# A hybrid attention and Mamba-2 decoder step in fp32: moving Pool's page loads and masks around the sample stage, and the order of products and DVE work at the scan's end and in the feed-forward openings

## What is computed

```python
for i in range(DEPTH):                       # DEPTH = 2
    hp, hs = rms_norm(xp, norm_mix[i]), rms_norm(xs, norm_mix[i])
    if i % N_MIXERS == 0:                    # native sparse attention
        yp, ... = nsa_layer(hp, 0, empty, ...)
        y_s, ... = nsa_layer(hs, past_len, past_c, past_s, cache_kv_win[l], ...)
    else:                                    # Mamba-2, chunked scan
        yp, ... = ssd_layer(hp, ...)
        y_s, ... = ssd_layer(hs, state_conv[l], state_ssm[l], ...)
    xp, xs = xp + yp, xs + y_s
    xp = xp + swiglu(rms_norm(xp, norm_ffn[i]), w_gate, w_up, w_down)
    xs = xs + swiglu(rms_norm(xs, norm_ffn[i]), w_gate, w_up, w_down)
```

## Time and profile before

| | before |
|---|---|
| median of 3 runs | 2317.47 us (2316.64 to 2322.97) |
| profiled execution | 2316.88 us |
| its span, granted clock of PE | 2315.2 us, 0.961 |
| busy: PE, weight loads, DVE, ACT, POOL | 2170.0, 1712.9, 1323.0, 519.2, 799.6 us |
| instructions | 33747 |
| moved by DMA | 236.59 MB, 102 GB/s in the mean |

### The profile page before, as it was taken

One profiled execution on the slowest core, in us unless ns is written; L12 is line 12 of the kernel. 1 busy time (PEld: TensorE's weight loads), 2 busy tenths in 40 slices (PEclk: granted clock), 3 DMA queues, 4 the chain that ended last, 5 costly groups with the idle time before them and its releaser, 6 DMA issues.

```text
span 2315.2 us, 33747 instructions
## 1 busy us (share of the span) xinstructions
PE 2170.0 (94%) x11958; PEld 1712.9 (74%) x11958; DVE 1323.0 (57%) x2172; ACT 519.2 (22%) x1197; POOL 799.6 (35%) x702
## 2 busy tenths in 40 slices
PE   8999899997898679999999999999987999999999
PEld 6867677875675457888887878887555878888877
DVE  4457788655774135556642178877986345556312
ACT  2202102104685212111100032233670021111000
POOL 3331000003002743434334245554882433434242
PEclk8999999987898889999999999999997999999999
DMA  4235433304013961711112312221431111122122
GB/s 170 73 110 155 131 119 105 115 13 147 19 38 107 346 231 55 253 74 73 73 50 100 123 61 73 81 85 61 164 147 52 76 73 73 73 89 83 50 77 87
DMA packets 87735, 236.59 MB, mean 102 GB/s; under 512 B 11441, under 2 KB 60722, under 8 KB 73234
## 3 DMA queue, kind: packets, MB, share of 16 engines
q1 hardware_dynamic: 66722, 191.97, 23.2%
q0 software_dynamic: 7024, 29.90, 3.9%
q10 hardware_dynamic: 13824, 12.59, 1.7%
HBM read 217.95 MB, written 23.73 MB: 104 GB/s over the span
## 4 chain that ended last, share of the span: by engine, by line
PE 74%; DVE 13%; issue 5%; POOL 2%; ACT 2%; POOLq 2%; SPq 1%; ACTq 0%; DMA 0%; DVEq 0%
PE ps L340 57%; PE ps L1008 6%; PE ps L1523 2%; PE ps L1536 1%; PE ps L1556 1%; POOLq L1840 1%; DVE sbuf L2534 1%; PE ps L921 1%; SPq L848 1%; PE ps L570 1%; PE ps L1411 1%; DVE sbuf L1156 1%; DVE sbuf L1165 1%; DVE sbuf L1164 1%; DVE sbuf L1162 1%
## 5 line engine op out<-in xcount | busy, mean ns | idle before, releaser
L340 PE MATMUL ps<-sbuf 128*128 128x272 f32 x6048 | 1414.6, 396 | 40.4 <-issue 11.1
L340 PEld LDWEIGHTS ps<-sbuf 128*128 128x128 f32 x6048 | 1156.6, 192 | 297.0 <-issue 20.6
L390 POOL TENSOR_TENSOR sbuf<-sbuf 128x512 f32<-128x512 f32 (+2 forms) x90 | 135.4, 1505 | 736.9 <-PE ps L340 521.7
L359 ACT ACTIVATE sbuf<-ps 128x272 f32<-128x272 f32 x180 | 71.6, 398 | 1118.0 <-PE ps L340 1086.2
L1008 PE MATMUL ps<-sbuf 128*128 128x256 f32 (+1 forms) x1280 | 298.0, 392 | 5.8 <-ACT sbuf L1086 5.0
L1008 PEld LDWEIGHTS ps<-sbuf 128*128 128x128 f32 x1280 | 243.7, 192 | 57.9 <-ACT sbuf L1086 5.4
L370 DVE TENSOR_TENSOR sbuf<-sbuf,ps 128x272 f32<-128x272 f32 x90 | 39.4, 438 | 252.4 <-PE ps L340 251.5
L399 POOL TENSOR_TENSOR sbuf<-sbuf 128x512 f32<-128x512 f32 (+2 forms) x90 | 142.0, 1577 | 7.8 <-PE ps L340 1.0
L396 POOL TENSOR_TENSOR sbuf<-sbuf 128x512 f32<-128x512 f32 (+2 forms) x90 | 136.2, 1513 | 12.3 <-DVE sbuf L407 5.3
L391 POOL TENSOR_TENSOR sbuf<-sbuf 128x512 f32<-128x512 f32 (+2 forms) x90 | 134.4, 1493 | 7.1
L378 DVE TENSOR_TENSOR sbuf<-sbuf,ps 128x272 f32<-128x272 f32 x90 | 39.4, 438 | 126.3 <-PE ps L340 125.5
(11 more groups left out here) (372 smaller groups left out, 2238.1 us busy)
## 6 DMA issues: line engine op xcount, KB each, us to landing
sbuf<-w_gu SPq DMA_DIRECT2D x44, 1024.0 KB, 4.9
sbuf<-w_down SPq DMA_DIRECT2D x32, 704.0 KB, 5.3
sbuf<-cmp_pages SPq DMA_DIRECT2D x160, 128.0 KB, 2.4
sbuf<-w_ssd_in SPq DMA_DIRECT2D x20, 1024.0 KB, 4.8
sbuf<-cmp_pages ACTq DMA_DIRECT2D x96, 128.0 KB, 3.0
sbuf<-w_nsa_in SPq DMA_DIRECT2D x9, 1024.0 KB, 4.9
sbuf<-sel_k SPq DMA_DIRECT2D x64, 128.0 KB, 2.7
sbuf<-sel_v SPq DMA_DIRECT2D x64, 128.0 KB, 4.7
```

Of the source, the lines that this page charges most:

```text
L340: last = pe.matmul(ps[:, bank_of(u, j), 0:HALF], a[:, kt * P:(kt + 1) * P], b[:, kt], start=kt == 0, stop=kt == kts - 1)
L359: do(act.activation(dst, bank_in(u, j), ACT.Copy), f_copied)
L390: do(pool.tensor_tensor(sv[:, 0], a21, a22, ALU.add), f_sums)
```

## The change

It moves work in eight places; the instructions are nearly all the same ones; one small ACT instruction, which loads a table, is new.

1. `p3_pool`: the V pages of sequence 1 are issued behind the compressed-score sums of tile 1, not ahead of them.
2. Sample stage: `comb` gets memory of its own, mask 0 is made before the meeting, the 16 issues of K pages of sequence 3 stand between meeting and memsets; the page numbers are read before the wait and not behind it; K pages of later pairs go ahead of window values on SP; the last constants are loaded earlier; in pair 0 DVE and ACT do the pages' scores ahead of the window's.
3. Feed-forward opening, both passes: (0, 0), (0, 1), (1, 0), (1, 1), and only then strips and (0, 2); POOL's sums wait for the later of products 3 and 4.
4. First down unit: slots released at product 4, not 6; product 4 and on wait for all four sums.
5. Entry of the scan: its first turns are made inside the last `ssd_in` unit, and the meeting there goes.
6. End of the scan: another order of DVE's work, all squares of the second half in one piece, and ACT's root table loaded ahead.
7. Banks of scan and `ssd_out` are numbered anew to fit.
8. `ssd_out`: product order (0, 0), (1, 0), (0, 1), (1, 1), (0, 4), (0, 6), (0, 3), (0, 5), (0, 2), and DVE makes the moving sums one kind after the other.

The diff, cut to its core:

```diff
         EARLY = [(0, 0), (0, 1), (1, 0), (1, 1)] + [(u, j) for u in range(2) for j in range(2, 7)]
-        early_at = {(U_SSD_OUT + u, j): n for n, (u, j) in enumerate(EARLY)}
+        EARLY_SSD = [(0, 0), (1, 0), (0, 1), (1, 1)] + [(0, j) for j in (4, 6, 3, 5, 2)] + [(1, j) for j in range(2, 7)]
+        early_at = {(u0 + u, j): n for u0, order in [(U_SSD_OUT, EARLY_SSD)] + [(u0, EARLY) for u0 in U_FFN]
+                    for n, (u, j) in enumerate(order)}
+        def pair_of(u):
+            return max(u0 for u0 in (U_SSD_OUT,) + U_FFN if u0 <= u)
         def bank_of(u, j):
             if u < U_NSA_OUT:
                 return (7 * u + j) % 6
             if (u, j) in early_at:
-                return (unit_at[U_SSD_OUT] + early_at[u, j]) % 8
-            return (unit_at[u] + j + (2 if j >= 2 and u in (U_NSA_IN, U_SSD_IN) + U_FFN else 0)) % 8
+                n = early_at[u, j]
+                return (unit_at[pair_of(u)] + n + (2 if n >= 4 and pair_of(u) in U_FFN else 0)) % 8
...
             if user is not None:
-                pool.wait_ge(f_mm, multiplied(user, 4))
+                pool.wait_ge(f_mm, max(multiplied(user, 3), multiplied(user, 4)))
...
-            pool.wait_ge(a_vev, 5)
-            pool.wait_ge(stored, 16)
-            p4_load_unit(pool, "V", 1)
             for i in range(1, QT):
                 pool.wait_ge(pc_low, added(i))
                 cmp_sloped(pool, pool_do)
                 cmp_shifted(pool, pool_do, i)
                 cmp_scaled(pool, pool_do, i)
-            meet(pool, 1)
+                if i == 1:
+                    pool.wait_ge(a_vev, 5)
+                    pool.wait_ge(stored, 16)
+                    p4_load_unit(pool, "V", 1)
...
             for pr in range(PAIRS - 1):
+                p4_load_unit(sp, "V", 2 * pr + 2, lambda: sp.wait_ge(ss_mm, pr + 1))
                 sp.wait_ge(sw_mm, pr + 1)
                 win_part(pr + 1, k_half, wk_in)
-                sp.wait_ge(ss_mm, pr + 1)
-                p4_load_unit(sp, "V", 2 * pr + 2)
-                sp.wait_ge(ss_pv, pr + 1)
+                if pr + 2 < PAIRS:
+                    p4_load_unit(sp, "K", 2 * pr + 4, lambda: sp.wait_ge(ss_pv, pr + 1))
+                else:
+                    sp.wait_ge(ss_pv, pr + 1)
                 win_part(pr + 1, v_half, wv_in)
-                if pr + 2 < PAIRS:
-                    p4_load_unit(sp, "K", 2 * pr + 4)
...
+            act.wait_ge(s_comb, 2)
+            def win_exp(pr):
                 act.wait_ge(sw_s, pr + 1)
                 act.activation(Sw, Sw, ACT.Exp, bias=few[:, 4, pr:pr + 1], scale=-1.0,
                                accum_out=few[:, 5, pr:pr + 1]).then_inc(sw_e, 1)
+            def exp(pr):
                 act.wait_ge(ss_s, pr + 1)
                 act.activation(S, S, ACT.Exp, bias=few[:, 8, pr:pr + 1], scale=-1.0,
                                accum_out=few[:, 9, pr:pr + 1]).then_inc(ss_e, 1)
+            for pr in range(PAIRS):
+                for part in (win_exp, exp) if pr else (exp, win_exp):
...
+            def mask(pr):
+                pool.tensor_tensor(comb.rearrange("p (s n) -> p s n", n=SELB), ali.rearrange("p (s n) -> p s n", n=SELB),
+                                   sel_bias[:, pr].unsqueeze(2).to_broadcast([P, NBLK, SELB]), ALU.add).then_inc(s_comb, 1)
+            pool.wait_ge(late_in, 32)
+            pool.wait_ge(sc_dve, SC_DVE["chosen"])
+            mask(0)
+            p4_load_unit(pool, "K", 3, lambda: meet(pool, 1))
             pool.memset(PT[:, NPAGE], 0.0).then_inc(zeroed, 1)
             pool.memset(PTw[:, 4], 0.0).then_inc(zeroed, 1)
             pool.wait_ge(zeroed, 7)
             pool.sem_inc(s_comb, 1)
-            pool.wait_ge(late_in, 16)
-            pool.wait_ge(sc_dve, SC_DVE["chosen"])
-            def mask(pr):
-                pool.tensor_tensor(comb.rearrange("p (s n) -> p s n", n=SELB), ali.rearrange("p (s n) -> p s n", n=SELB),
-                                   sel_bias[:, pr].unsqueeze(2).to_broadcast([P, NBLK, SELB]), ALU.add).then_inc(s_comb, 1)
-            mask(0)
-            p4_load_unit(pool, "K", 3)
             for pr in range(PAIRS - 1):
-                pool.wait_ge(ss_mm, pr + 1)
-                p4_load_unit(pool, "V", 2 * pr + 3)
+                p4_load_unit(pool, "V", 2 * pr + 3, lambda: pool.wait_ge(ss_mm, pr + 1))
                 pool.wait_ge(ss_s, pr + 1)
                 mask(pr + 1)
                 if pr + 2 < PAIRS:
-                    pool.wait_ge(ss_pv, pr + 1)
-                    p4_load_unit(pool, "K", 2 * pr + 5)
+                    p4_load_unit(pool, "K", 2 * pr + 5, lambda: pool.wait_ge(ss_pv, pr + 1))
...
+                    elif v == GU_UNITS and j >= 3:
+                        pe.wait_ge(f_sums, 4 * u + (2 if j == 3 else 4))
+                    elif j == 3:
+                        pe.wait_ge(f_sums, 4 * u + 4)
+                    first = product(pe, u, j, a, b, KH if gu else FH, before)
+                    if j == (4 if v == GU_UNITS else 3) and (v % 2 or not gu):
+                        first.then_inc(w_used, 2 if gu else 4)
+                for v, j in EARLY:
+                    one(v, j)
+                for v in range(2, UNITS_L):
+                    for j in range(7):
+                        one(v, j)
...
+                    if i == ZS + XS - 1 and j == 3:
+                        step_turns(pe)
...
-            group_squares_on(pe, 1, (0, 1))
+            group_squares_on(pe, 1, range(GROUPS))
...
+                if t == N_STEPS:
+                    do(act.activation(cbm_s[:, 0:1], eps, ACT.Sqrt))
...
+            gate(H0_SPREAD - 1)
+            take_state(H0_SPREAD - 1)
+            normed(0)
+            take_y(H0_SPREAD)
+            gate(H0_SPREAD)
+            take_state(H0_SPREAD)
+            normed(1)
+            normed(2)
+            invert_on(dve, do, 1)
+            normed(3)
...
-            invert_on(dve, do, 1)
+            def scaled_half(j):
+                if j % 4 == 0:
+                    dve.wait_ge(g_sp, GROUPS + j // 4 + 1)
+                do(dve.scalar_tensor_tensor(xc[:, j, n2], xc[:, j, n2], ssm_norm[:, j:j + 1],
+                                            ps[:, root_bank(j // 4), 0:HALF], ALU.mult, ALU.mult), g_out)
+            los, his = [xc[:, kt] for kt in range(KT)], [xc[:, KT + kt] for kt in range(KT)]
+            for kt, lo in enumerate(los):
+                scaled_half(kt)
+                do(dve.tensor_tensor(y_t1[:, kt], lo[:, n2], lo[:, n1], ALU.subtract), f_turns)
             for kt in range(KT):
-                for j in (kt, KT + kt):
-                    dve.wait_ge(g_sp, GROUPS + j // 4 + 1)
-                    do(dve.scalar_tensor_tensor(xc[:, j, n2], xc[:, j, n2], ssm_norm[:, j:j + 1],
-                                                ps[:, root_bank(j // 4), 0:HALF], ALU.mult, ALU.mult), g_out)
-                lo, hi = xc[:, kt], xc[:, KT + kt]
-                do(dve.tensor_tensor(y_t1[:, kt], lo[:, n2], lo[:, n1], ALU.subtract))
-                do(dve.tensor_tensor(y_t2[:, kt], hi[:, n2], y_t1[:, kt], ALU.subtract))
+                scaled_half(KT + kt)
+            for kt, hi in enumerate(his):
+                do(dve.tensor_tensor(y_t2[:, kt], hi[:, n2], y_t1[:, kt], ALU.subtract), f_turns)
+            for lo, hi in zip(los, his):
+                do(dve.tensor_tensor(lo[:, n2], hi[:, n2], lo[:, n2], ALU.subtract), f_turns)
+            for kt, hi in enumerate(his):
                 do(dve.tensor_tensor(y_t4[:, kt], hi[:, n1], y_t2[:, kt], ALU.subtract), f_turns)
...
             one(0, 0, half_ready(0))
-            group_squares_on(pe, 1, (2, 3))
-            one(0, 1, half_ready(1))
             for g in range(GROUPS):
-                kt = 4 * (g % 2) + 3
-                claim(pe, root_bank(g), g_out, ST + 2 * kt + 1 + g // 2)
+                claim(pe, root_bank(g), g_out, ST + 4 * g + 4)
             pe.wait_ge(n_r, 5)
             for g in range(GROUPS):
                 pe.matmul(ps[:, root_bank(g), 0:HALF], row_strip(g, 0).to_broadcast([32, P]), rstd[quarter(g), n2],
                           start=True, stop=True).then_inc(g_sp, 1)
             one(1, 0)
+            one(0, 1, half_ready(1))
             one(1, 1)
-            one(0, 2, lambda kt: pe.wait_ge(f_turns, TURNS_BEFORE["ssd_out"] + kt + 1))
-            for i in range(4):
+            one(0, 4, turn_ready(0))
+            one(0, 6, half_ready(3))
+            one(0, 3, turn_ready(1))
+            one(0, 5, turn_ready(2))
+            one(0, 2, turn_ready(3))
+            for i in range(1, 4):
                 for j in range(2 if i < 2 else 0, 7):
-                    if (i, j) != (0, 2):
-                        one(i, j)
+                    one(i, j)
```

236 lines of the change are left out of this document (121 added, 115 removed).

## The result

| | before | changed |
|---|---|---|
| median of 4 runs | 2317.05 us (2314.20 to 2322.97) | 2281.11 us (2277.12 to 2284.75) |
| profiled execution, its span | 2316.88, 2315.2 us | 2280.75, 2279.1 us |
| granted clock | 0.961 | 0.968 |
| busy PE, DVE | 2170.0, 1323.0 us | 2155.7, 1346.0 us |

The ratio is 0.9847, 95% interval 0.9829 to 0.9865: faster by 36 us. The forecast was 2264.2, range 2252 to 2280. The direction is right, the size is two thirds of what was forecast, and the median lies 1 us above the range.

A forecast was written before the change was run, and what follows sets the result against it. The prediction took the kernel to be bound by PE's matmuls, with gains only where PE idles or its clock is low. Its terms summed to -52.7 us from the profiled 2316.88, giving 2264.2 us, range 2252 to 2280.

The forecast's parts named there:

- Sample stage: Four pairs of page and window work: earlier masks gain, pair 0 pays; net -4.4 us, bounds -8 and +3.
- the step on SP's queue: Sample stage: SP issues K pages ahead of window values, costing nothing if the values still land before their products.
- Rival B: Sample stage bound by its loads: the 4.4 us gain is lost, late window values cost 6 more; 2274.6 us, chance 0.14.
- The pair 0 step: Sample stage, pair 0: K issues delay DVE's start, and page turns start 2.2 us later; +2.2 us.
- +1.7 for the last three moving sums held beside POOL: Output projection: DVE's last sums are held by POOL's unit 1 sums; +1.7 us, or +4.6 with DVE 3 us late.
- prompt attention: V issues move behind tile 1's sums, so DVE's 9.87 us idle goes; -9.9 us, bounds 9.0 to 10.4.
- both openings: Feed-forward openings: waits for moving and weight sums are covered; -6.4 us first pass, including 2.7 low clock, -3.7 second.
- both down units: First down unit, each pass: earlier slot release removes PE's wait for POOL's last weight sum; -4.3 and -5.2 us.
- entry: Entry of the scan: turns move into the last unit and PE's 1.9 us meeting wait goes; -2.0 us.
- scan's end up to the root spread: DVE's second inversion moves into the scan's end, bringing the root spread earlier; -12.2 us of the -16.8 term.
- C: Scan's end gives back half: low clock costs 9.4 us, longer holds beside POOL 2.9; 2276.5 us, chance 0.14.
- D: Down units gain nothing: slots free earlier but weights come no sooner, so 9.5 us stay; 2273.7 us, chance 0.06.

The follow-up runs named there:

- run 4: Changed kernel with the three edits of run 1, run 2 and run 3 together: 2265.57 us, ratio to before 0.9782.
- run 1: Changed kernel with SP issuing each window half ahead of the sixteen page transfers again, page numbers still read early: 2275.76 us.
- run 5: Changed kernel with the edits of run 1 and run 2, and window halves of pairs 1 to 3 cut to 16 columns: 2271.48 us, one execution.
- run 2: Changed kernel with POOL's memsets and signal to DVE and ACT directly behind the meeting, ahead of the 16 K issues: 2277.17 us.
- run 3: Changed kernel with POOL's weight sums for unit 1 of the output projection made behind all of DVE's moving sums: 2276.54 us.
- run 12: Changed kernel with POOL's four weight sums for unit 1 of the output projection replaced by eight memsets: 2278.16 us, one execution.
- run 10: Changed kernel with the old product order in the feed-forward openings, products still waiting for two, two, three and four sums: 2283.67 us.
- run 7: Changed kernel with POOL's V pages of sequence 1 issued ahead of the compressed sums again: 2291.39 us.
- run 8: Changed kernel with the first down unit's ring slots released at product 6 and its products waiting for sums as before: 2287.53 us.
- run 9: Changed kernel with feed-forward openings as before: unit 0 whole, then unit 1, all four weight sums ahead of product 3: 2287.73 us.
- run 11: Changed kernel with PE's first scan products waiting until DVE has written the last pair of gate blocks: 2280.00 us.
- run 6: As run 4, but products 3 to 6 of output projection unit 1 wait for two, two, three and four weight sums: 2266.06 us.

## Why the prediction was right and wrong

**Sample stage: wrong in the step on SP's queue.** "That costs nothing if the values still land before their products" was the condition, and it did not hold: PE waits 2.34 and 3.00 us for values. Worse, the step named only the K pages that went ahead of window values. The V pages of the same pair went ahead of the window's K half as well, which the diff shows in the same loop, and PE waits 3.24 and 1.22 us for these. The reading of page numbers went ahead of both halves too, about 5 us each time, and the forecast counted it only as a gain for POOL. SP's queue should have been written out issue by issue. So pairs 1 and 2, forecast at -0.4 and -3.1, came at +1.5 and +3.0. The stage of 107.2 us that the forecast gave is what run 4 has, but only with the signal ahead as well, which the forecast did not have; with the halves first alone (run 1) it is 110.8. Rival B had the mechanism (its second half, 6 us late halves, 2274.6) but was given 0.14; its first half, the rate, is disproved by run 5. The pair 0 step was right to 0.1 us in its sum, with two deviations that cancel, and it was a cost that nothing needed: run 2 takes it away, and more.

**Behind the root spread: the mechanism right, the size off.** The mis-sized term was +1.7 for the last three moving sums held beside POOL. Measured were 8 us of holding in the last sixteen and 3 in the first two, and run 3, which takes away the 8, is 6.2 us shorter up to unit 1's product 2: the term cost 6.2. I had the two sizes in view: with DVE 3 us late "it would be +4.6". What I did not do is to ask what makes DVE late: POOL's first set of sums, which stood beside the first blocks in the changed order (POOL starts it when the state's store has landed, after 6.54 us idle). Behind the spread PE came when forecast and POOL 1 us later, but DVE was 3.8 us late with its first kind already. The 3 us of slack went to the first blocks and the third kind, and the holds of the fourth kind then went to PE, with slow records behind each wait. Rows said so: the earlier trace rows gives the price, and each two-input operation of a stretch counts, not just the last. Run 3 and run 12 show the cause from both sides; that the first set alone uses up the slack is worked out, no run takes it away. Run 3 has no hold in the last sums and still takes the 33.0 us that the forecast had with 1.7 of holding in it. So 1.7 more were missing: the root spread's own 1.07 us stood nowhere in the sum, the eight products took 30.84 us and not 30.4, and the wait for ACT's copy 1.06 and not 0.9.

**Inside the scan, and the end of compression: not in the sum.** +2.4 and +2.8. The second is for the most part the clock on unchanged code. Of the first, 1.7 lies ahead of DVE's first take of a state. Measured from the last add of the last but one `ssd_in` unit, that take comes after 66.2 us before, after 65.7 to 65.8 in the changed kernel and eight of its runs, and after 63.7 in runs 1, 4 and 10, whose code is the same there. The clock goes with it: 0.50 from 1610 to 1614 in the changed kernel, 1.00 at the same steps of run 4. So this is scatter too. The other 0.7 was not taken apart, and its cause is open.

**Right**: prompt attention (-9.9, measured -10.8), both openings in sum (-10.1, -10.7), both down units (-9.5, -9.4), entry (-2.0, -2.1), scan's end up to the root spread (-12.2, -13.7). In each of these a named wait of the chain had a cover that was priced by its own rows. The first four were taken back by runs 7 to 11; for the scan's end, the largest term, only the rows speak. Its -13.7 is a lucky profile: from DVE's ninth take of a state to the root spread the same code takes 28.5 us in the changed kernel and 31.6 in runs 3, 6, 10 and 12, its first 7 us in run 3 at a granted clock of 0.67 and not 1.00. By those it would be -10.6, and the forecast lies between. In the opening the 2.7 us of low clock stood in the first pass, because the profile before had them there; run 9 shows that they belong to no pass, so that this term fits because both sides are read against the same profile.

**The range** was left by 1.1 us, which is less than the +5.2 of the two stretches that were not in the sum and are mostly scatter. B, C and D were each placed alone in it; 8.3 of B's 10.4 and 6.3 of C's 12.3 came together, 14.6 us. With these alone the time would have been 2278.8, inside the range, so which side of 2280 it fell on was luck; the two terms were wrong either way.

## What to carry to other kernels

When a change moves page loads ahead of something, write the queue down issue by issue and ask of each transfer behind the moved ones when its reader comes; a half that lands 3 us late gives back what the mask had gained. When DVE's adds with two inputs in SBUF are put beside POOL's weight sums, price each of them by up to one POOL operation, from the first one on, or wait with POOL's sums until DVE is through: here one wait was worth 5 us. Before an opening is reordered, ask whether the product needs all the sums that it waits for; that was three quarters of this one, the low clock behind the longer wait included.

## What the runs showed of the hardware that I had not expected

- Whether an idle time of PE is followed by a low clock changes from run to run for the same instructions: behind 3.76 us of waiting the clock was 0.56 in the first pass and 1.00 in the second before, and 1.00 and 0.50 in run 9. It is worth 3 us each time, as much as many edits, so a profile's total should be split at marks before two kernels are compared.
- POOL's reading operations held DVE for up to a whole operation (1.90 us for a 0.44 us add), memsets of the same tile did not hold it at all. It is not only adds with two inputs: an operation with a single SBUF input and a constant (L465) takes 0.50 us alone, and 3.29 beside one of POOL's sums in the changed kernel and in each of its runs:

```profile
1217.41 3.29 DVE L465 TENSOR_SCALAR sbuf<-sbuf 128x544 f32<-128x544 f32 x1
...
1216.88 3.52 POOL L402 TENSOR_TENSOR sbuf<-sbuf 128x1408 f32<-128x1408 f32 x1
```

In run 3 another took 2.47 beside POOL's last sum:

```profile
1771.13 2.47 DVE L465 TENSOR_SCALAR sbuf<-sbuf 128x544 f32<-128x544 f32 x1
```

Whether a memset holds such an operation too is open.

- Sixteen issues by page number took 9.3 us on POOL's queue and 8.2 to 11.3 on SP's, and reading the sixteen numbers about 5 us more. What stands behind them in the queue is that much later.
